# Six more up tiles in seven block products, three transfers moved, and unread products in the selection: a two-block transformer kernel on one core

## The chip, the cores and the metric

The kernel runs on one core of one Trainium2 chip. The metric is the device time of one execution in microseconds (us); a few runs are taken and their median stands for the kernel. A profiled execution gives the trace, and its own time stands beside its span below.

## The reference, cut to what matters

Two transformer blocks one after the other, in float32, on 256 tokens of width 1024. The change lies in the feed-forward part of the first block (two layers) and in the expert selection of the second block (two layers).

```python
# first block, for each of two layers
mod = silu(c) @ w_mod[layer] + b_mod[layer]           # shift, scale and gate vectors, 6 x 1024
h = rmsnorm(x, g_mlp[layer]) * (1 + scale2) + shift2
up = h @ w_up[layer]                                  # 1024 -> 2 x 2816
u, g = up[..., :2816], up[..., 2816:]
g = causal_depthwise_conv(g, conv_w[layer], conv_b[layer])   # three taps along the tokens
x = x + gate2 * ((silu(g) * u) @ w_down[layer])
...
# second block, for each of two layers
aff = softmax(x @ w_router + b_router)                # 16 experts
gate, idx = top_k(aff.T, 32)                          # each expert takes 32 tokens
```

## The kernel before, in words

**Engines.** Each engine runs its own list of instructions in order and waits on semaphores. TensorE (PE) multiplies, VectorE (DVE) and ScalarE (ACT) do the elementwise work, GpSimd (POOL) does some sums, SyncE (SP) issues nearly all transfers.

**Tiles and the ring.** Weights come from memory in tiles of up to 2 MB into a ring of six slots. `_b1_tiles` (line 83) writes the order of the first block's tiles. Before each transfer, SyncE waits until the tile six places ahead in this order has been used (`sp.wait_ge(tile_done, t + 1)`, behind line 680); `tile_done` counts used tiles in the same order, and TensorE raises it. So the place of a tile in the order sets the earliest moment of its transfer. Three transfers are no tiles and stand at fixed places of this loop: the bias copies (line 676) and the router weights (line 678) ahead of up tile 4, and the second layer's attention gate bias (line 682) ahead of up tile 8. SyncE issues in order, and the transfers share one queue.

**Up tiles.** The up projection has eleven tiles a layer. A tile holds 256 columns of `u` and 256 of `g`, and moves in two transfers of 1 MB. A *whole* tile is 32 products of 128x128 weights with 128x256 of the stream, each two instructions in float32 (`up`, line 1266). In the second layer tiles 2 to 10 are multiplied in *seven block products* in place of eight (`up_seven`, line 1304): 56 products of 128x128 with 128x128. These need sums. GpSimd makes the first and third weight sums (`up_sums`, lines 2221 and 2223), VectorE the second (`up_second`, 2790) and the fourth (`up_fourth`, 2796), and once a layer the sums of the stream's rows (`up_rows_sums`, 2779 to 2784). ScalarE copies block 1 out of PSUM (`up_copies`, 1918) and VectorE joins the other six (`up_join`, 2810 to 2816). `UP_WHOLE = (11, 2)` says how many tiles of each layer are whole.

**Convolution.** For each up tile VectorE makes the last tap with its bias (2759) and adds the other two taps (2764), ScalarE takes silu (1927), VectorE multiplies with `u` (2771). That last step is `b1_product_ready`; TensorE waits for it before it overwrites a PSUM bank or reads the product.

**Modulation tiles.** Each of `w_mod`'s tiles (2 MB) is reduced on VectorE by `accumulate` in eight steps (one of line 2381, seven of line 2384, 128x512 each), then summed over partitions by TensorE in `modulation` (line 900 for gates, 903 for the others), and read by `mod_out` (2401, 2403). Sums alternate between two buffers. In the first layer, modulation tiles 10 to 21 follow one each upon up tiles 2 to 10 and down tiles 0 to 2 (`LAGS`): VectorE sums tile 10 + j after product j, and TensorE multiplies it behind up tile j + 2.

**Down tiles.** The down projection has six tiles, also in seven products (line 1332). VectorE makes all its sums (`down_sums`, 2828 to 2837). Tiles 3, 5 and 4 end it together, and their second product needs the sums of all three.

**Selection.** In the second block (second loop over layers), TensorE turns the router's result into logits (`logits`, 1561) and transposes the affinities (`flip_affinity`, 1567). VectorE then finds the 32 largest in four rounds (3175, 3177) and forms slot numbers (3182, 3185), which TensorE transposes (1601, 1603); VectorE copies them (3187). `warm` (line 1573) writes products that nothing reads to a PSUM bank; five stand in these waits before the change, and one behind.

The order on SyncE around the moved transfers:

```python
for t, (L, kind, j) in enumerate(B1_TILES):
    if (L, kind, j) == (0, "up", 4):
        sp.dma_start(copies...)      # bias copies, 2.7 MB
        sp.dma_start(router...)      # 128 KB in rows of 64 bytes
    if (L, kind, j) == (0, "up", 8):
        sp.wait_ge(sems["b1_mix_added"], 4)
        sp.dma_start(gates...)       # 512 KB
    sp.wait_ge(tile_done, t + 1)     # the tile six places ahead is used
```

## Time and profile before

| what | value |
|---|---|
| median of three runs | 1941.82 us (1941.79 to 1944.37) |
| the profiled execution's own time | 1944.36 us |
| its span | 1942.6 us |
| TensorE matmul busy | 1657.2 us (85%) |
| VectorE busy | 708.4 us (36%) |
| ScalarE busy | 283.5 us (15%) |
| GpSimd busy | 143.7 us (7%) |
| bytes read from memory | 594.76 MB |
| TensorE begins the first layer's up stage | 184.92 us |
| one half of a whole up tile (128 of the 256 tokens) | 7.14 us |
| eight transposes of the stream between two halves | 0.87 us |
| first block | 0 to about 769 us |
| second block's experts | from about 924 and from about 1509 us |

In a chain of waits each row is one stretch of work that released the next: its start, its length, and the engine, name and line. A timeline row has start, length, engine, line, operation, shapes and count, and in brackets the idle time before it with what ended it. A windows row gives for each stretch its length, each engine's busy time with instructions, the granted clock (1.00 is 2.4 GHz, 0.50 is 1.2 GHz), the share of time for which the 16 transfer engines were busy, and the rate. PE is TensorE's matmul, PEld its weight loads, SPq SyncE's queue of issues.

### The profile page before, as it was taken

To read this page: it belongs to the slowest core of one execution; us is meant where nothing else is said; L and a number is where in the kernel's file an instruction comes from. 1 tells how busy PE (TensorE), PEld (TensorE's weight loads), DVE (VectorE), ACT (ScalarE), POOL (GpSimd) and SP (SyncE) were. 2 spreads that over 40 slices of the span, in tenths; PEclk is the share of its full clock that TensorE was granted. 3 is DMA by queue.
4 is the path that set the end of the run, shared out by engine and by line. 5 is a ranking of instruction groups with operands and counts; after the bars stand their busy time and mean duration, and the time that the engine had idled before them with its cause. 6 is when DMAs were issued, how large, how long until landed. Compare 5 with 4: busy or idle time off the path is not lost.

```text
span 1942.6 us, 24583 instructions
## 1 busy us (share of the span) xinstructions
PE 1657.2 (85%) x10484; PEld 945.1 (49%) x10484; DVE 708.4 (36%) x1470; ACT 283.5 (15%) x761; POOL 143.7 (7%) x151
## 2 busy tenths in 40 slices
PE   8999999999999999999785766758999785756757
PEld 3455988544579964474432232322574432232322
DVE  1584566977528976273010010101174110010101
ACT  1243000021511001252000010001253000010000
POOL 0011000000213510310000000000220000000000
PEclk9999999999999999999897887979999997987978
DMA  9991888755235643646999999999845999999998
GB/s 353 328 350 59 261 292 298 277 202 187 88 110 187 233 152 125 201 174 241 402 428 430 428 432 425 433 429 409 266 174 216 404 429 430 426 432 427 432 429 352
DMA packets 165957, 599.76 MB, mean 309 GB/s; under 512 B 20977, under 2 KB 79857, under 8 KB 142065
## 3 DMA queue, kind: packets, MB, share of 16 engines
q1 hardware_dynamic: 165630, 598.04, 78.4%
q8 instruction: 61, 1.00, 0.2%
q10 hardware_dynamic: 242, 0.53, 0.1%
q14 instruction: 24, 0.19, 0.0%
HBM read 594.76 MB, written 3.80 MB: 308 GB/s over the span
## 4 chain that ended last, share of the span: by engine, by line
PE 57%; DMA 38%; DVE 3%; ACT 2%; issue 1%; POOL 0%; SPq 0%; DVEq 0%; ACTq 0%
DMA extra<-in_w_down 14%; DMA extra<-in_w_up 12%; DMA extra<-in_w_gate 11%; PE ps L1266 9%; PE ps L1379 6%; PE ps L1332 6%; PE ps L1304 5%; PE ps L1625 5%; PE ps L949 4%; PE ps L1118 4%; PE ps L1517 3%; PE ps L1216 3%; PE ps L1645 1%; DMA ring<-in_w_mod 1%; PE ps L835 1%; PE ps L857 1%
## 5 line engine op out<-in xcount | busy, mean ns | idle before, releaser
L1625 PE MATMUL ps<-ring,wide 128*32 128x256 f32 x2912 | 219.7, 468 | 117.4 <-DMA ring<-in_w_up 72.4
L1625 PEld LDWEIGHTS ps<-ring,wide 128*32 128x32 f32 x2912 | 107.7, 133 | 223.2 <-DMA ring<-in_w_up 81.8
L1645 PE MATMUL ps<-ring,wide 128*32 128x512 f32 x768 | 157.4, 638 | 45.7 <-DMA ring<-in_w_down 45.7
L3212 DVE TENSOR_TENSOR wide<-ps,wide 128x512 f32<-128x512 f32 x16 | 10.7, 670 | 508.8 <-PE ps L1625 508.8
L1266 PE MATMUL ps<-hT,ring 128*128 128x256 f32 (+1 forms) x1088 | 183.8, 330 | 0.0
L1266 PEld LDWEIGHTS ps<-hT,ring 128*128 128x128 f32 x1088 | 166.6, 191 | 17.3 <-issue 2.9
L1625 PE MATMUL ps<-extra,wide 128*32 128x256 f32 x1056 | 91.4, 519 | 63.6 <-DMA extra<-in_w_up 38.7
L1379 PE MATMUL ps<-ring,hT 128*128 128x512 f32 (+2 forms) x320 | 127.3, 555 | 0.4 <-issue 0.4
L1645 PEld LDWEIGHTS ps<-ring,wide 128*32 128x32 f32 x768 | 44.7, 116 | 154.4 <-issue 126.4
L2384 DVE SCALAR_TENSOR_TENSOR extra<-ring,sc,extra 128x512 f32<-128x512 f32 x140 | 109.8, 785 | 5.2
L1625 PEld LDWEIGHTS ps<-extra,wide 128*32 128x32 f32 x1056 | 42.9, 147 | 111.0 <-DMA extra<-in_w_up 42.5
L1379 PEld LDWEIGHTS ps<-ring,hT 128*128 128x128 f32 x320 | 60.3, 190 | 62.2 <-issue 53.4
L949 PE MATMUL ps<-ring,hT 128*128 128x512 f32 x192 | 86.6, 606 | 0.9 <-ACT hT L1771 0.9
L2153 ACT ACTIVATE wide<-ps 128x512 f32<-128x512 f32 x8 | 4.8, 597 | 560.8 <-PE ps L1645 420.2
L3225 DVE COPY wide<-ps 128x512 f32<-128x512 f32 x8 | 5.5, 692 | 203.1 <-PE ps L1645 202.5
L2232 POOL TENSOR_TENSOR sc<-sc,tab 128x1 f32<-128x1 f32 (+1 forms) x18 | 24.5, 1370 | 621.2 <-DVE sc L2329 589.6
L1304 PE MATMUL ps<-hT,ring 128*128 128x128 f32 x576 | 68.7, 275 | 0.0
L1304 PEld LDWEIGHTS ps<-hT,ring 128*128 128x128 f32 x576 | 66.6, 192 | 1.0 <-issue 1.0
L1332 PE MATMUL ps<-ring,wide 128*128 128x512 f32 x136 | 61.6, 595 | 0.0
L1573 PE MATMUL ps<-tab 128*128 128x512 f32 (+1 forms) x116 | 58.5, 643 | 1.2 <-DVE spare L3177 1.2
L949 PEld LDWEIGHTS ps<-ring,hT 128*128 128x128 f32 x192 | 36.3, 193 | 44.8 <-issue 43.4
L1517 PE MATMUL ps<-ring,hT 128*128 128x512 f32 x128 | 56.6, 595 | 0.9 <-ACT hT L2084 0.9
(373 smaller groups left out, 2098.6 us busy)
## 6 DMA issues: line engine op xcount, KB each, us to landing
ring<-in_w_gate SPq DMA_DIRECT2D x24, 4096.0 KB, 31.4
ring<-in_w_down SPq DMA_DIRECT2D x24, 4096.0 KB, 33.6
ring<-in_w_up SPq DMA_DIRECT2D x20, 4096.0 KB, 32.9
ring<-in_w_mod SPq DMA_DIRECT2D x24, 2048.0 KB, 13.4
ring<-in_w_up SPq DMA_DIRECT2D x44, 1024.0 KB, 8.0
extra<-in_w_gate SPq DMA_DIRECT2D x8, 4096.0 KB, 35.1
extra<-in_w_up SPq DMA_DIRECT2D x8, 4096.0 KB, 33.1
ring<-in_w_in SPq DMA_DIRECT2D x13, 2048.0 KB, 12.6
```

Of the source, the lines that this page charges most:

```text
L949: last = mm(ps[bank1(i, c)][:, 0:w], h8[:, k, c * P:(c + 1) * P], wt[:, k, 0:w], start=k == 0, stop=k == KD - 1)
L1118: last = mm(ps[in_bank(m, r)][:, :], lhs[:, g, :], rhs[:, g, :], start=g == 0, stop=g == 3)
L1216: last = mm(ps[OUT_BANK[c, n]][:, :], h8[:, k, c * P:(c + 1) * P], wt[:, k, :], start=k == 2, stop=k == 7)
L1266: last = mm(ps[2 * (j % 2) + half][:, f * T + o:f * T + o + n], wt[:, k, w:w + P], h8[:, k, o:o + n], start=k == 0, stop=k == KD - 1)
L1304: last = mm(ps[UP_BANK[m]][:, half * P:(half + 1) * P], lhs[:, g, half, :], rhs[:, g, :], start=g == 0, stop=g == 3)
L1332: last = mm(ps[DOWN_BANK[m]][:, :], lhs[:, g, :], rhs[:, g, :], start=begin and j == tiles[0] and g == 0, stop=end and j == tiles[-1] and ...
L1379: last = mm(ps[2 * (i % 2) + c][:, 0:w], h8[:, k, c * P:(c + 1) * P], wt[:, k, 0:w], start=k == 0, stop=k == KD - 1)
L1517: last = mm(ps[bank][:, :], h8[:, at_, c * P:(c + 1) * P], wt[:, k, :], start=k == parts[0][0], stop=k == parts[-1][0])
L1573: mm(ps[bank][:, 0:cols_], ident, tab[:, 0:cols_], start=True, stop=True)
L1625: last = mm(ps[2 * part + e // 2][j * CAP:(j + 1) * CAP, e % 2 * 2 * P:(e % 2 + 1) * 2 * P], xsT[:, k, e * CAP:(e + 1) * CAP], expert_row( ...
L1645: last = mm(ps[6 + n][e * CAP:(e + 1) * CAP, :], hidT[:, e, k, :], expert_row(n0, e, k)[:, n * N:(n + 1) * N], start=k == 0, stop=k == KD - 1)
L2384: stt(acc[:, q % 2, :], wt[:, k, :], csil[:, k:k + 1], acc[:, q % 2, :], ALU.mult, ALU.add)\
```

## The change

- `UP_WHOLE` becomes `(5, 2)`: up tiles 5 to 10 of the first layer go in seven products as in the second. The functions that were for the second layer alone take the layer as a parameter; GpSimd's `up_sums` stands ahead of the router's gains now.
- The first tap with its bias goes from VectorE (two instructions of line 2759) to ScalarE (`tap`, two activations with scale and bias), in both layers. `conv(j)` is left with four VectorE instructions. In a step of seven products `conv(j - 1)` stands ahead of the joins of tile j.
- At the first seven-product tile the second weight sum comes ahead of the row sums, and both ahead of the convolution of the tile before.
- Modulation tiles of the first layer get new places in the order (`FOLD_AFTER`), sums at new places on VectorE (10 to 13 in the residual stretch, then `SUM_WHOLE`, `SUM_FIRST`, `SUM_PARTS`), reads at new places (`READ_AFTER`), three sum buffers in place of two, and other PSUM banks.
- The bias copies and router weights are issued ahead of up tile 8, not 4; the gate bias ahead of up tile 2, not 8.
- Three unread products are added to each selection.

```diff
-UP_WHOLE = (11, 2)
+UP_WHOLE = (5, 2)
+FOLD_AFTER = ({("out", 1): (10, 11), ("up", 1): (12, 13), ("up", 2): (14, 15), ("up", 3): (16,), ("up", 4): (17, 18),
+               ("up", 7): (19,), ("up", 9): (20,), ("down", 2): (21,)}, {("up", 6): (0,), ("up", 7): (1,)})
+READ_AFTER = ({1: (12, 13), 2: (14, 15), 3: (16,), 8: (19,), 10: (20,)}, {6: (0,), 7: (1,)})
+SUM_WHOLE = {0: (14,), 1: (15,), 2: (16, 17), 3: (18,)}
+SUM_FIRST = ({5: (19, range(0, 2)), 6: (19, range(4, 6)), 7: (20, range(0, 2)), 8: (20, range(4, 6))}, {})
+SUM_PARTS = ({5: (19, range(2, 4)), 6: (19, range(6, 8)), 7: (20, range(2, 4)), 8: (20, range(6, 8))},
...
-                if (L, kind, j) == (0, "up", 4):
+                if (L, kind, j) == (0, "up", 8):
                     sp.wait_ge(sems["rpb_loaded"], 16)
...
-                if (L, kind, j) == (0, "up", 8):
+                if (L, kind, j) == (0, "up", 2):
                     sp.wait_ge(sems["b1_mix_added"], 4)
...
                         elif m == 5:
-                            pe.wait_ge(*s.at("b1_product_ready", 2))
+                            pe.wait_ge(*s.at("b1_product_ready", first - first % 2))
+                        elif m == 3:
+                            pe.wait_ge(*s.at("b1_product_ready", first - 1 + first % 2))
...
                 route(1, range(4, KD)).then_inc(s.up("b2_router_done"), 1)
+                warm(7, 1, T)
                 pe.wait_ge(*s.at("b2_logits_ready", 1))
                 logits(1)
                 flip_affinity(0)
+                warm(7, 1)
+                warm(7, 1, P)
                 flip_affinity(1)
...
+                def tap(j):
+
+                    y = sm[:, j % 2, :].rearrange("p (f t) -> p f t", f=2)
+                    act.wait_ge(*up_block(s, L, 4, j))
...
+                    for f in range(2):
+                        av(y[:, f, :], gp[:, f, :], ACT.Identity, scale=cc1(L, "conv_w", 2 * FCH + 2 * j + f),
+                           bias=cc1(L, "conv_b", 2 * j + f)).then_inc(s.up("b1_up_by_act" if f else None), 1)
...
                 out_residual(0, 0)
+                if L == 0:
+                    accumulate(10)
                 out_residual(0, 1)
                 norm_stream(which, 0)
                 out_residual(1, 0)
                 evac_stream(which, 0, 24)
+                if L == 0:
+                    accumulate(11)
                 out_residual(1, 1)
                 norm_stream(which, 1)
                 evac_stream(which, 1, 24)
+                if L == 0:
+                    accumulate(12)
+                    mod_out(10)
+                    accumulate(13)
+                    mod_out(11)
...
+                first = UP_WHOLE[L]
+                for j in range(first - 1):
+                    conv(j)
+                    up_gated(j)
+                    if L == 0:
+                        for q in SUM_WHOLE[j]:
+                            accumulate(q)
+                up_second(first)
+                up_rows_sums()
                 if L == 0:
-                    mod_out(EARLY[L] + UPT - LAGS[L])
+                    mod_out(17)
+                    mod_out(18)
+                for j in range(first, UPT):
+                    if j in SUM_FIRST[L]:
+                        accumulate(*SUM_FIRST[L][j])
+                    conv(j - 1)
+                    up_join(j, UP_READS[:1])
+                    up_fourth(j)
+                    up_gated(j - 1)
+                    if j in SUM_PARTS[L]:
+                        accumulate(*SUM_PARTS[L][j])
+                    if j == UPT - 1:
+                        down_sums(0)
+                    up_join(j, UP_READS[1:])
+                conv(UPT - 1)
+                up_gated(UPT - 1)
+                down_sums(1)
                 down_sums(2)
                 down_sums(3)
                 if L == 0:
-                    accumulate(EARLY[L] + UPT)
-                    mod_out(EARLY[L] + UPT + 1 - LAGS[L])
+                    accumulate(21)
```

## Rows read from the trace of the kernel before

**Rows 1.** The page: the span, and its 40 slices of transfers (share busy, rate)
```profile
span 1942.6 us, 24583 instructions
...
DMA  9991888755235643646999999999845999999998
GB/s 353 328 350 59 261 292 298 277 202 187 88 110 187 233 152 125 201 174 241 402 428 430 428 432 425 433 429 409 266 174 216 404 429 430 426 432 427 432 429 352
```

**Rows 2.** Chain of waits, first layer's up and down stage (start us, us, what)
```profile
242.87 0.86 PE ps L900 x2
243.72 13.81 PE ps L1266 x64
257.54 0.79 PE ps L903 x8
...
346.49 12.23 PE ps L1332 x28
...
371.73 0.42 DVE extra L2828
...
393.99 20.87 PE ps L1332 x48
```

**Rows 3.** Timeline of TensorE, second layer's first seven-product tiles
```profile
585.10 3.74 PE L1304 MATMUL ps<-hT,ring 128*128 128x128 f32 x32
...
594.35 2.05 PE L1304 MATMUL ps<-extra 128*128 128x128 f32 x16 [1.27 <-DVE wide L2771]
...
599.81 3.74 PE L1304 MATMUL ps<-hT,ring 128*128 128x128 f32 x32
...
612.32 3.74 PE L1304 MATMUL ps<-hT,ring 128*128 128x128 f32 x32
```

**Rows 4.** Timeline of SyncE's issues, first layer
```profile
189.98 17.79 SPq L678 DMA_DIRECT2D router<-in_w_router  x1
207.82 3.06 SPq L705 DMA_DIRECT2D ring<-in_w_up  x2
```

**Rows 5.** Windows of the first layer (busy us, clock, transfer share, GB/s)
```profile
187.00:198.00 11.00, 11.00 (x101) 11.00 (x100) 2.28 (x6) 2.92 (x7) 0.54 (x1) 1.00 1.06 372
198.00:208.00 10.00, 10.00 (x92) 10.00 (x91) 0.73 (x2) 0.00 (x0) 0.00 (x0) 1.00 0.93 262
208.00:212.00 4.00, 4.00 (x39) 4.00 (x38) 3.20 (x8) 0.63 (x1) 0.57 (x1) 1.00 0.58 94
245.00:256.00 11.00, 11.00 (x53) 9.68 (x52) 7.66 (x12) 0.63 (x1) 0.00 (x0) 1.00 1.03 361
```

**Rows 6.** Windows of the first selection
```profile
909.90:913.40 3.50, 1.62 (x6) 0.62 (x6) 2.09 (x11) 2.41 (x4) 0.00 (x0) 0.97 1.00 424
913.40:920.20 6.80, 6.27 (x8) 2.62 (x9) 4.88 (x21) 3.32 (x3) 0.00 (x0) 0.51 1.00 422
```

**Rows 7.** Timeline, both selections: unread products and VectorE's wait behind them
```profile
913.93 6.72 PE L1573 MATMUL ps<-tab 128*128 128x512 f32 x8 [0.59 <-DVE spare L3177]
...
921.02 0.19 DVE L3187 COPY sc<-ps 128x32 f32<-128x32 f32 x1 [2.43 <-PE ps L1603]
...
1506.30 0.19 DVE L3187 COPY sc<-ps 128x32 f32<-128x32 f32 x1 [0.85 <-PE ps L1603]
```

**Rows 8.** Timeline of VectorE, second layer's seven-product tiles
```profile
587.97 1.22 DVE L2790 TENSOR_TENSOR extra<-extra,ring 128x1024 f32<-128x1024 f32 x1
589.29 1.00 DVE L2759 TENSOR_SCALAR spare<-ps,fixed 128x256 f32<-128x256 f32 x2
...
614.47 1.79 DVE L2764 SCALAR_TENSOR_TENSOR spare<-extra,fixed,spare 128x255 f32<-128x255 f32 x4
...
616.63 1.23 DVE L2796 TENSOR_TENSOR ring<-ring,extra 128x1024 f32<-128x1024 f32 x1
```

**Rows 9.** Groups of VectorE: modulation steps, 599.8 to 700, then 200 to 340 us
```profile
L2384 DVE SCALAR_TENSOR_TENSOR extra<-ring,sc,extra 128x512 f32<-128x512 f32 x14 | 15.0, 1075 | 0.7
...
L2384 DVE SCALAR_TENSOR_TENSOR extra<-ring,sc,extra 128x512 f32<-128x512 f32 x68 | 51.2, 753 | 2.4
```

More of the change, by code:

```diff
@@ L90, in _b1_tiles @@
                 tiles += [(0, "mod", q) for q in MOD_AT[i]]
-        tiles += [(l, "out", j) for j in range(2)]
-        late = MODS[l][EARLY[l]:]
-        steps = [(l, "up", j) for j in range(UPT)] + [(l, "down", j) for j in range(NDOWN)]
-        for n, t in enumerate(steps):
+        tiles.append((l, "out", 0))
+        for t in [(l, "out", 1)] + [(l, "up", j) for j in range(UPT)] + [(l, "down", j) for j in range(NDOWN)]:
             tiles.append(t)
-            if LAGS[l] <= n < len(late) + LAGS[l]:
-                tiles.append((late[n - LAGS[l]][0], "mod", late[n - LAGS[l]][1]))
+            tiles += [(MODS[l][q][0], "mod", MODS[l][q][1]) for q in FOLD_AFTER[l].get(t[1:], ())]
     return tiles
@@ L124, with _up_acts @@
 TAB = {}
+def _up_acts(l):
+    first = UP_WHOLE[l]
+    acts = [(what, j) for j in range(first - 1) for what in ("tap", "silu")]
+    for j in range(first, UPT):
+        acts += [("tap", j - 1), ("copy", j), ("silu", j - 1)]
+    return acts + [("tap", UPT - 1), ("silu", UPT - 1)]
+UP_ACTS = [_up_acts(l) for l in range(DEPTH)]
+UP_SEVEN = [UPT - UP_WHOLE[l] for l in range(DEPTH)]
 def _tab():
@@ L1317, in _ @@
                         up(j, 0, T)
-                    if 0 <= j - LAGS[L] < late:
-                        modulation(EARLY[L] + j - LAGS[L])
+                    folds(("up", j))
                 pe.wait_ge(*s.at("b1_product_ready", UPT - 1))
@@ L1349, in _ @@
                     last.then_inc(tile_done, 1)
-                    if UPT + j - LAGS[L] < late:
-                        modulation(EARLY[L] + UPT + j - LAGS[L])
+                    folds(("down", j))
                 for j in DOWN_TAIL:
@@ L1927, in _, with up_copies @@
                     av(pT[:, j % 2, :], sm[:, j % 2, :], ACT.Silu).then_inc(s.up("b1_up_by_act"), 1)
+                def up_copies(j):
+                    act.wait_ge(*up_block(s, L, 1, j))
+                    if j >= UP_WHOLE[L] + 2:
+                        act.wait_ge(*s.at("b1_product_ready", j - 1))
+                    for c in range(2):
+                        av(up_joined(j)[:, :, 0, c * P:(c + 1) * P], ps[UP_BANK[1]][:, 0:T].rearrange("p (h t) -> p h t", h=2),
+                           ACT.Copy).then_inc(s.up("b1_up_by_act" if c else None), 1)
+                for what, j in UP_ACTS[L]:
+                    if what == "tap":
+                        tap(j)
+                    elif what == "silu":
+                        silu(j)
+                    else:
+                        up_copies(j)
                 if L == DEPTH - 1:
@@ L2389, in mod_out @@
                     t = B1_AT[(l, "mod", i)]
-                    b = MOD_BANK if L or t > B1_AT[(L, "down", 0)] else 7 - q % 2 if q in MOD_AT[LAST_IN] else 4 + q % 2
+                    b = mod_bank(L, q)
                     if L == 0 and q < FAST:
@@ new lines, in _ @@
+                if L == 0:
+                    mod_out(17)
+                    mod_out(18)
+                for j in range(first, UPT):
+                    if j in SUM_FIRST[L]:
[9 more added lines that the diff above has]
+                    up_join(j, UP_READS[1:])
```

207 lines of the change are left out of this document (96 added, 111 removed).

## The prediction

> **What bounds the kernel now.** Read the page first: the span is 1942.6 us and the row of transfers is at its ceiling only in the two stretches in which the experts' weights stream; the first 900 us are not filled by them [rows 1]. So a microsecond saved ahead of 900 us moves the whole stream to the left. The second view is the chain of waits over the first layer's up and down stage: it is TensorE without a gap to the end of the second down tile, one whole up tile (line 1266) being 13.81 us, with a modulation product of 0.86 or 0.79 us between two tiles; only at 371.73 does VectorE take over, until TensorE starts again at 393.99 [rows 2]. The third is the timeline of the second layer, where tiles of the same size already go in seven products: in steady state one takes 612.32 - 599.81 = 12.51 us [rows 3]. The fourth is what feeds the first layer: SyncE's issues and the rate of the transfers [rows 4, 5]. The last is the selection, where unread products run at half the full clock [rows 6, 7].
>
> The profiled execution took 1944.36 us, 1.8 more than its span; the median of the runs is 1941.82, 2.5 less. Differences of span are put on the median. 0.2% of it, 3.9 us, is about what a measurement can tell from no change.
>
> **The change, part by part.** *Six tiles in seven products.* 13.81 - 12.51 = 1.3 us [rows 2, 3], times six is 7.8 us less TensorE. ScalarE's copy and taps, GpSimd's sums and VectorE's joins come on top; what they cost is whether they are late, below.
>
> *Modulation tiles 19 and 20.* Their products move from behind down tiles 0 and 1 into the up stage: 0.79 us each, no difference in the sum. Taken alone the up stage would end 7.8 - 1.6 = 6.2 us earlier, at 340.3 where it was 346.49 [rows 2].
>
> *The down stage.* VectorE's last sums end at 393.99, 47.5 us after the stage begins; they restart when down tile 1 is done, 25.2 us in, because two modulation products lie before that [rows 2]. Without them two tiles of 12.1 us make 24.3, so this chain ends some 1.0 us earlier relative to the stage's start. Modulation sum 21 stays in it, so the stall of 2 to 3 us before 393.99 stays: VectorE is late next, as before.
>
> *Sums 10 to 13 ahead of the convolutions.* Each is eight steps, 6.0 us, on VectorE in the residual and norm stretch, where it mostly waits for TensorE. TensorE's clock of the new stage, from the table: 184.92 + 7.14 + 0.87 (transposes) + 7.14 = 200.1, modulation products 10 and 11 to 201.8, two more half tiles to 216.1, products 12 and 13 to 217.6. VectorE has sums 12 and 13 and their reads done at about 208.4, up tile 0 ends at 208.9, and taps, silu and product take some 4 us: product 0 comes at 213 and tile 2 wants it at 217.6; tile 2's own transfer lands near 209. Cost nothing; if the cover is gone, each sum costs 6.0 us at most.
>
> *The transfers.* This is where I expect most of the gain to go. A transfer waits until the tile six places ahead in the order is done. In the new order tile 2 of up waits for modulation tile 10, which TensorE finishes at about 201, and from there the queue does not run dry: up 2, modulation 14, 15, up 3, 16, up 4, 17, 18, up 5, 6, 7, 19 are all released before the queue reaches them. A pair of an up and a modulation tile (4.2 MB) moves at 361 to 372 GB/s [rows 5], so a tile takes 5.65 to 5.8 us; with a late end on some of the 16 engines it may be 6.2. I take 5.75. From 202.3, twelve tiles put modulation tile 19 at 271. VectorE wants its first two steps at the head of the step of up tile 5, before conv 4, the first join and the fourth sum. From landing to the fourth sum are two steps (1.3 us) and the stretch 614.47 to 617.86 of the second layer [rows 8]: 4.7 us, and product 4 0.6 more. TensorE starts tile 5 at 217.6 + 3 x 13.8 + 4.1 (five modulation products) = 263.1 and wants both 9 us into it, at 272; it gets them at 276 to 277. **Stall one: 4 us.**
>
> Behind tile 19 come the bias copies and the router weights, which the change puts ahead of up tile 8. Before, they sat right ahead of the transfer issued at 207.82: the queue moved at 262 GB/s and then at 94 GB/s for the 14 us from 198 to 212, and SyncE's issue of the router took 17.79 us, so everything behind it on SyncE waits too [rows 4, 5]. Then up 8, up 9 and modulation tile 20: 14 + 3 x 5.75 = 31 us after tile 19. Tile 20 lands at about 302.5 (301 by the fast rate, 309 by the slow one). Tile 6 ends at 263.1 + 2 x 12.5 + 4 = 292.1; VectorE is through its joins and reaches modulation 20's first two steps (ahead of conv 6) at 293 to 294 and stands in order behind the wait: conv 6, join and fourth sum of tile 7 are queued there, and TensorE waits for that sum at 300 to 301. It gets it at 302.5 + 4.7 = 307.2. **Stall two: 6 us.** From there to the down stage no other transfer is late: two products of tile 7 (3.6 us), three tiles of 12.5, two modulation products of 0.8. The down stage then starts at 307.2 + 3.6 + 37.5 + 1.6 = 349.9, against 346.49: 3.4 later instead of 6.2 earlier. With the 1.0 of the down stage, **the first layer loses 2.4 us**. By the fast rate it loses 1, by the slow one 9; with no backlog at all it wins 7.2.
>
> The gate transfer (0.5 MB) moves ahead of up 2 and lies in the queue before 202: nothing.
>
> *Layer two.* ScalarE now makes the first tap, and the order is second sum, row sums, conv 1 instead of row sums, second sum, conv 1. Seven-tile 2 took 599.81 - 585.10, 2.2 us over the steady 12.51, and the one large wait in it is for product 1 [rows 3, 8]. Taking out the second sum (1.2) and the two taps (1.0) brings product 1 to 592.1, where TensorE wants it at 592.2. **Minus 2.2**, and nothing else in that layer changes on TensorE. ScalarE's two taps (some 1 us) are late by a fraction only at the last tile, where line 1332 wants product 10 with 2 us to spare.
>
> *Selection.* Between 909.9 and 913.4 TensorE is busy 1.62 of 3.5 us at a granted clock of 0.97; in the 6.8 us after that the granted clock is 0.51, that is 1.2 GHz, and four unread products (eight instructions) last 6.72 us. VectorE waits 2.43 us for the product behind them; in the second selection 0.85 us [rows 6, 7]. The change adds unread products of 256 columns ahead of the second logits and 512 and 128 ahead of the second flip, some 1.5 us at 2.4 GHz, in gaps of 0.5 and 1.4 us. If the clock holds, the waits shrink to the 0.55 us that the two small products need: **minus 1.9 and minus 0.3**. They hide in the gaps; at 1.2 GHz they would cost 0.8 us a selection instead. The bounds are therefore -2.2 and +1.6. I take -2.2, since the activity ahead of the fall nearly doubles.
>
> By the Trainium skill ("TensorE: Matmul & The Clock Gate", The HAM clock gate) the gate judges activity on its own free-running timing, not on the program's. By that rule shifting the program can move the fall to other instructions whatever the added products do, and the sum would be 2.2 us less good. No row here shows one execution with another phase.
>
> Sum: 2.4 - 2.2 - 2.2 = -2.0 us, **1939.8 us**.
>
> **VectorE beside GpSimd.** In the second layer the fourteen modulation steps of line 2384 last 1075 ns in the mean where, without GpSimd at work, they last 753 [rows 9]. The new steps lie where GpSimd has paused, so I price them at 0.8; at 1.075, a tile of the first layer with four steps fills VectorE for some 13 us against 12.5, 0.5 us each for four tiles, 2 us at most. The Trainium skill ("SBUF — State Buffer", Who interferes with whom) says that a VectorE instruction with two inputs in SBUF and a reading GpSimd one exclude each other for the whole instruction. The trace's mean agrees.
>
> **The rivals.**
> A. *The transfers are in time.* If transfers overlap better than one after another, tile 20 lands before 296 and only stall one or nothing is left. Then the first layer wins 3.2 to 7.2, and the whole 8 to 12: 1930 to 1934. For it: the page's rate reaches 430 GB/s in the experts' stretch [rows 1]. Against: no stretch with these packets is above 372 [rows 5]. Chance 0.22.
> B. *The queue falls further behind, slower than before.* One mechanism, at VectorE's wait for modulation tile 20 ahead of conv 6. Each microsecond that it lands after 302.5 is one on the path. At 304.5 the gain is gone, and from 308.5 the kernel is over 0.2% slower. With 6.2 us a tile and 16 us for copies and router it lands at 309 to 310: first layer +9.5, total +5, 1947. For it: every 2 MB counts from the slowest of the 16 engines, and landings are later than the mean rate says. Against: gaps in the release let the slow engine catch up. Chance 0.20.
> C. *The clock does not hold* and all else as forecast: 1942.0, or 1943.6 with the added products in the way. Chance 0.18.
> The forecast itself, within 3 us: 0.40.
>
> **How the numbers follow.** Most of A, and the part of the forecast in which tile 20 lands by 300.5, is faster by over 0.2%: 0.36. The slower half of B with a clock that does not hold gives 0.19. The rest, 0.45, is no difference. The range takes the forecast, C, most of B and the nearer part of A: 1931.5 to 1947.
>
> **What would show it.** A TensorE tile of 12.5 us in the first layer and two long ones, of 16 to 17 us (up 5) and 18 (up 7); VectorE idle before line 2384's step, released by the transfer of a modulation tile, twice; transfer share near 1 from 202 to 300; the router's issue after 261; tile 2 of the second layer at 12.5 us; VectorE's wait before line 3187's copy at 0.6 us in both selections. The forecast is wrong if the down stage starts before 346 or after 353, or if the granted clock falls in the selection.

## The result, and the profile after

The changed kernel takes **1952.91 us**, median of five runs (1949.92 to 1953.8), beside 1944.08 us for the kernel before in the same comparison. The ratio is 1.0047, 95% interval 1.0036 to 1.0058: slower by 0.47%, some 9 us, outside the range of the prediction. The profiled execution took 1953.05 us with a span of 1951.0, 8.4 more than the 1942.6 of before, so the two profiles carry the whole difference.

It is easiest to find by milestones of TensorE, the moments at which it begins a stage. The columns are the profile before, the profile after, what the stretch gained or lost, and what the prediction had for it.

| stretch | before | after | difference | forecast |
|---|---|---|---|---|
| first layer's down stage begins | 346.35 | 355.14 | +8.8 | +3.4 |
| from there to its last group of blocks | 70.1 | 68.9 | -1.15 | -1.0 |
| from there to the second layer's up stage | 139.2 | 142.5 | +3.3 | 0 |
| second layer's nine seven-product tiles | 116.8 | 116.2 | -0.5 | -2.2 |
| all behind the first block, the selections in it | 1175.4 | 1173.5 | -1.9 | -2.2 |

The last group of the down stage is at 416.43 before and 424.07 after, the up stage at 555.64 and 566.58. The stretches not listed are equal to 0.01 us. The sum is +8.4, and against the forecast's -2.0 it leaves 10.4 us to explain: 5.4 in the first row, 3.3 in the third, 1.7 in the fourth. The first row counts from the start of the span, and executions of one kernel come to the up stage at different times: 184.76 us in the profile before, 183.96 in the one after, 181.3 to 184.0 in the four profiles of the kernel after. From the first up tile to the down stage are 161.6 us before and 171.2 after: the stage itself is 9.6 us longer.

The page's row of transfers is as full as the forecast has it: the fifth slice of the rates has 344 GB/s where it had 261, the sixth 320 where it had 292 [rows 1].

```profile
span 1951.0 us, 25339 instructions
...
DMA  9992996545325742744999999999944999999998
GB/s 352 334 341 75 344 320 238 194 168 194 124 87 174 248 165 86 244 173 197 402 431 428 425 433 426 432 430 410 288 173 199 406 427 432 425 431 427 432 430 351
```

TensorE's timeline of the first layer has the forecast's two long tiles. Up tile 5 begins at 263.71, tile 7 at 297.59; in each the sixth block waits for VectorE. The bracket is the idle time.

```profile
261.01 1.02 PE L940 MATMUL ps<-extra,tab 128*128 128x512 f32 x2
262.79 1.05 PE L943 MATMUL ps<-tab,extra 128*128 128x1 f32 x8 [0.77 <-DVE extra L2454]
263.71 3.82 PE L1355 MATMUL ps<-hT,ring 128*128 128x128 f32 x32
...
270.94 1.95 PE L1355 MATMUL ps<-extra 128*128 128x128 f32 x16
278.61 3.78 PE L1355 MATMUL ps<-hT,ring 128*128 128x128 f32 x16 [5.72 <-DVE wide L2845]
282.18 3.07 PE L1355 MATMUL ps<-extra,ring 128*128 128x128 f32 x16
285.09 3.74 PE L1355 MATMUL ps<-hT,ring 128*128 128x128 f32 x32
...
297.59 3.74 PE L1355 MATMUL ps<-hT,ring 128*128 128x128 f32 x32
...
310.56 2.60 PE L1355 MATMUL ps<-hT,ring 128*128 128x128 f32 x16 [3.87 <-DVE ring L2870]
312.96 3.04 PE L1355 MATMUL ps<-extra,ring 128*128 128x128 f32 x16
...
355.14 1.02 PE L1382 MATMUL ps<-ring,wide 128*128 128x512 f32 x2
```

A group of 16 products that elsewhere begins 1.79 us before its successor takes 3.57 and 2.91 us behind the first stall, 2.40 and 2.87 behind the second. The windows say why: the granted clock, 0.93 and 1.00 in the two gaps themselves, is at its lower level (0.50, 1.2 GHz) for most of both stretches behind them.

```profile
278.60:285.10 6.50, 6.49 (x33) 6.49 (x34) 4.67 (x8) 0.00 (x0) 0.00 (x0) 0.54 0.75 158
310.50:316.00 5.50, 5.44 (x35) 5.47 (x35) 5.02 (x8) 0.00 (x0) 1.04 (x1) 0.69 0.00 0
```

Against 1.79 for a group that is 2.9 us lost behind the first stall and 1.7 behind the second. What VectorE did ahead of the second stands in its own timeline, with GpSimd's below it:

```profile
303.33 0.48 DVE L2451 TENSOR_SCALAR extra<-ring,sc 128x512 f32<-128x512 f32 x1 [4.66 <-DMA ring<-in_w_mod]
303.86 0.75 DVE L2454 SCALAR_TENSOR_TENSOR extra<-ring,sc,extra 128x512 f32<-128x512 f32 x1
304.52 3.68 DVE L2838 SCALAR_TENSOR_TENSOR spare<-extra,fixed,spare 128x255 f32<-128x255 f32 x4
308.13 0.41 DVE L2890 TENSOR_TENSOR extra<-ps,extra 128x256 f32<-128x256 f32 x1
308.57 1.84 DVE L2870 TENSOR_TENSOR ring<-ring,extra 128x1024 f32<-128x1024 f32 x1
...
```

```profile
305.05 2.87 POOL L2280 TENSOR_TENSOR extra<-ring 128x512 f32<-128x512 f32 x2 [6.29 <-PE ps L1355]
307.89 3.65 POOL L2282 TENSOR_TENSOR ring<-ring 128x512 f32<-128x512 f32 x2
```

Modulation tile 20 landed at 303.3 (forecast 302.5). But the four taps took 3.68 us, not the 1.79 of [rows 8], and the fourth sum 1.84, not 1.23; TensorE's block could start at 310.6 instead of 307.2. Behind the first stall's landing the same four taps ran beside GpSimd's sums too, which were at work from 271.25 to 276.88. There they read PSUM and not two tiles of SBUF, the on-chip memory, and took what they take alone:

```profile
274.45 1.77 DVE L2838 SCALAR_TENSOR_TENSOR spare<-ps,fixed,spare 128x255 f32<-128x255 f32 x4
```

In the selection the rows that answer to [rows 6] and [rows 7] have a full clock, and eight product instructions last 4.37 us, not 6.72:

```profile
922.00:928.00 6.00, 5.11 (x13) 1.60 (x12) 5.33 (x26) 5.14 (x4) 0.00 (x0) 1.00 0.99 421
```

```profile
921.05 1.24 PE L1618 MATMUL ps<-tab 128*128 128x512 f32 x4
...
924.32 4.37 PE L1618 MATMUL ps<-tab 128*128 128x512 f32 x8 [0.59 <-DVE spare L3247]
```

### The profile page after: what moved, and what is told of

The parts are those of the page before. It is cut to its first block, busy times and chain, and to the rows that moved or that the text cites. A ratio compares the mean times of both kernels' runs of the same rounds, so it can differ in the third digit from the quotient of the medians.

```text
span 1951.0 us, 25339 instructions
## 1 busy us (share of the span) xinstructions
PE 1654.6 (85%) x10784; PEld 951.7 (49%) x10784; DVE 736.6 (38%) x1484; ACT 310.1 (16%) x817; POOL 178.9 (9%) x175
## 4 chain that ended last, share of the span: by engine, by line
PE 52%; DMA 38%; DVE 5%; ACT 2%; SPq 1%; issue 1%; POOL 0%; DVEq 0%; ACTq 0%
DMA extra<-in_w_down 14%; DMA extra<-in_w_up 12%; DMA extra<-in_w_gate 11%; PE ps L1424 6%; PE ps L1355 6%; PE ps L1382 6%; PE ps L1673 5%; PE ps L1306 5%; PE ps L989 4%; PE ps L1158 4%; PE ps L1562 3%; PE ps L1256 3%; DMA ring<-in_w_mod 2%; PE ps L1693 1%; DVE extra L2454 1%
## 5 line engine op out<-in xcount | busy, mean ns | idle before, releaser
L1355 PE MATMUL ps<-hT,ring 128*128 128x128 f32 x960 | 117.3, 279 | 9.6 <-DVE wide L2845 5.7
L1355 PEld LDWEIGHTS ps<-hT,ring 128*128 128x128 f32 x960 | 113.1, 195 | 10.9 <-DVE wide L2845 5.9
L1306 PE MATMUL ps<-hT,ring 128*128 128x128 f32 (+1 forms) x704 | 100.1, 304 | 0.0
L1306 PEld LDWEIGHTS ps<-hT,ring 128*128 128x128 f32 x704 | 94.1, 191 | 6.7 <-issue 1.9
L2454 DVE SCALAR_TENSOR_TENSOR extra<-ring,sc,extra 128x512 f32<-128x512 f32 x112 | 95.1, 849 | 4.5
L989 PE MATMUL ps<-ring,hT 128*128 128x512 f32 x192 | 86.6, 606 | 0.9 <-ACT hT L1819 0.9
L2280 POOL TENSOR_TENSOR extra<-ring 128x512 f32<-128x512 f32 x30 | 43.6, 1474 | 194.0 <-PE ps L1355 126.8
L1618 PE MATMUL ps<-tab 128*128 128x512 f32 (+2 forms) x128 | 59.3, 590 | 1.2 <-DVE spare L3247 1.2
```

The source lines that it names most:

```text
L989: last = mm(ps[bank1(i, c)][:, 0:w], h8[:, k, c * P:(c + 1) * P], wt[:, k, 0:w], start=k == 0, stop=k == KD - 1)
L1306: last = mm(ps[2 * (j % 2) + half][:, f * T + o:f * T + o + n], wt[:, k, w:w + P], h8[:, k, o:o + n], start=k == 0, stop=k == KD - 1)
L1355: last = mm(ps[UP_BANK[m]][:, half * P:(half + 1) * P], lhs[:, g, half, :], rhs[:, g, :], start=g == 0, stop=g == 3)
L1618: mm(ps[bank][:, 0:cols_], ident, tab[:, 0:cols_], start=True, stop=True)
L2454: stt(total, wt[:, k, :], csil[:, k:k + 1], total, ALU.mult, ALU.add)\
```

## The experiments

Sixteen runs follow: twelve changed kernels and four repetitions of the kernels before and after. The theory at the start: two stalls of TensorE at VectorE's waits for modulation tiles 19 and 20, each with a stretch of half clock behind it. The rival: transfers or VectorE's load set the pace, and the place of the waits does not matter. The main readings of the profiles are in one table at the end of this section.

**The copies and the router later** (`e1_router_late`).

```diff
-                if (L, kind, j) == (0, "up", 8):
+                if (L, kind, j) == (0, "down", 0):
```

> Kernel after, with the two transfers (bias copies, router) sent ahead of down tile 0 instead of up tile 8. Theory (two stalls, each followed by a stretch at half clock): modulation tile 20 lands some 14 us earlier, the second stall (3.9 us at 310.6) and the 1.8 us that its blocks took longer go, the first stall (5.7 us and 3.1 us) stays: 5 to 6 us less than after, 1.0015 to 1.002 of before. Rival (the queue is only behind somewhere else): the down tiles then come late, the down stage waits and the time stays at after's.

1946.83 us, ratio 1.0022 (1.0013 to 1.0032): 6 us under after, the larger end of what was expected. The second stall is gone and the first, now 6.73 us, stays. Tile 20 is there when VectorE wants it, and the taps behind it take their usual time, because they are over before GpSimd starts its next sums at 303.85:

```profile
298.69 1.79 DVE L2838 SCALAR_TENSOR_TENSOR spare<-extra,fixed,spare 128x255 f32<-128x255 f32 x4
```

So the slow taps of the kernel after come of the wait: the late tile pushes them onto GpSimd's sums.

**The sums behind the first join** (`e2_sums_behind_join`).

```diff
-SUM_FIRST = ({5: (19, range(0, 2)), 6: (19, range(4, 6)), 7: (20, range(0, 2)), 8: (20, range(4, 6))}, {})
+SUM_FIRST = ({}, {})
-SUM_PARTS = ({5: (19, range(2, 4)), 6: (19, range(6, 8)), 7: (20, range(2, 4)), 8: (20, range(6, 8))},
+SUM_PARTS = ({5: (19, range(0, 4)), 6: (19, range(4, 8)), 7: (20, range(0, 4)), 8: (20, range(4, 8))},
```

> Kernel after, with the sums of modulation tiles 19 and 20 that stood at the head of VectorE's part of seven-product tiles 5 to 8 put behind the first join of the same tile (four steps there instead of two and two). Theory: VectorE no longer stands in front of a transfer with the taps and the fourth sum behind it, so both stalls of TensorE go with their slow clock: 5.7 + 3.1 + 3.9 + 1.8 = 14.5 us less than after, some 1940 us (0.997 of before), less if the two parts not split make the joins late. Rival (the lost time is VectorE's load and the collision with GpSimd, not the place of the wait): the stalls move to the joins, at most 4 us less than after.

1950.53 us, ratio 1.0035 (1.0020 to 1.0049). The rival is right. The two long stalls go and six short ones come, at the second or the fourth sum of tiles 6 to 9, 7.8 us together:

```profile
282.13 2.02 PE L1355 MATMUL ps<-spare,extra 128*128 128x128 f32 x16 [1.05 <-DVE extra L2864]
288.59 2.02 PE L1355 MATMUL ps<-hT,ring 128*128 128x128 f32 x16 [0.86 <-DVE ring L2870]
...
298.24 2.74 PE L1355 MATMUL ps<-spare,extra 128*128 128x128 f32 x16 [2.27 <-DVE extra L2864]
...
313.99 2.02 PE L1355 MATMUL ps<-spare,extra 128*128 128x128 f32 x16 [0.49 <-DVE extra L2864]
```

The granted clock falls again behind the two waits of 2.27 us (0.64 and 0.65 over the next 5 us), which makes these tiles longer still. Four steps of a sum behind the join are more than VectorE has room for. Two ahead of the taps and two behind the join do fit as long as the tile has landed: in `e1_router_late` up tiles 6 to 8 have four steps each and take 12.5 us. Ahead of the taps the two steps stand in the 1.2 us in which VectorE otherwise waits for ScalarE's first tap, and before GpSimd's sums.

**Both edits** (`e3_both`).

> Both edits. Theory: no more than e2 alone, since either cure removes the second stall, and e2 the first too: within 2 us of e2. Rival (the transfers themselves bound the up stage, their 98 per cent share of the queue): e3 is faster than e2 by 4 us or more, for up tiles 8 and 9 come 10 us earlier.

1951.38 us, ratio 1.0043 (1.0030 to 1.0057), the same as `e2_sums_behind_join` within the intervals. With the four steps together behind the join VectorE's work binds, wherever the router stands.

**The selection alone** (`e4_before_plus_products`). The kernel before, with only the three unread products.

```diff
+                warm(7, 1, T)
                 pe.wait_ge(*s.at("b2_logits_ready", 1))
                 logits(1)
                 flip_affinity(0)
+                warm(7, 1)
+                warm(7, 1, P)
```

> Kernel before, with only the three unread products of the selection. Theory: the granted clock holds behind the first selection, 1.9 us there and 0.3 in the second layer: 2.2 us less than before, ratio 0.9989. Rival: the products only fill the wait and the clock falls all the same, ratio 1.000.

1941.93 us, ratio 0.9993 (0.9983 to 1.0002): 2.1 us less, as expected, though the interval reaches 1. The clock row decides: 1.00 through the stretch that answers to [rows 6]. Of the eighteen profiles of this study the sixteen with the three products have no fall in the first selection, the two without have one. This part of the change works, but what it gives depends on the execution: 1.9 us against the profile of before that the prediction read, 0.7 against its repetition (below).

**Sums spread three to a tile, tile 20 back in the down stage** (`f1_spread`). On top of the first experiment's edit:

```diff
-               ("up", 7): (19,), ("up", 9): (20,), ("down", 2): (21,)}, {("up", 6): (0,), ("up", 7): (1,)})
+               ("up", 8): (19,), ("down", 1): (20,), ("down", 2): (21,)}, {("up", 6): (0,), ("up", 7): (1,)})
-SUM_FIRST = ({5: (19, range(0, 2)), 6: (19, range(4, 6)), 7: (20, range(0, 2)), 8: (20, range(4, 6))}, {})
+SUM_FIRST = ({}, {})
-SUM_PARTS = ({5: (19, range(2, 4)), 6: (19, range(6, 8)), 7: (20, range(2, 4)), 8: (20, range(6, 8))},
+SUM_PARTS = ({6: (19, range(0, 3)), 7: (19, range(3, 6)), 8: (19, range(6, 8))},
...
                 down_sums(1)
+                if L == 0:
+                    accumulate(20)
                 down_sums(2)
                 down_sums(3)
                 if L == 0:
                     accumulate(21)
+                    mod_out(20)
```

> Kernel after with three edits in the first layer: the bias copies and the router ahead of down tile 0; modulation tile 19 taken after up tile 8 instead of 7, its eight steps put behind the joins of tiles 6, 7 and 8 as 3, 3 and 2; modulation tile 20 taken after down tile 1, with its sums behind the second down sums, where the kernel before has them. Theory (VectorE was both waiting at transfers and, at four steps of a sum in each tile, full): neither stands now, the six tiles take 12.5 us each and the down stage starts at 339 to 342 us instead of 346.5 before and 355.3 after; with the selection's 2.2 us the whole is 8 to 10 us under before, ratio 0.995 to 0.996. Rival (the saturated transfers bound the up stage in any order): TensorE waits at up tiles 8 to 10 by name of the weights, the down stage starts at 347 or later, ratio 0.999 or more.

**1937.88 us, ratio 0.9974 (0.9964 to 0.9983)**: faster than before, by 5.6 us where 8 to 10 were expected (its profiled execution has 7.7 us less span). In the profile the down stage starts at 339.55, as expected; no tile waits, each takes 12.5 us:

```profile
276.12 3.74 PE L1355 MATMUL ps<-hT,ring 128*128 128x128 f32 x32
...
288.63 3.74 PE L1355 MATMUL ps<-hT,ring 128*128 128x128 f32 x32
...
301.14 3.74 PE L1355 MATMUL ps<-hT,ring 128*128 128x128 f32 x32
```

**The same, and the second layer's modulation tile 11 a tile later** (`f2_spread_both`).

```diff
-{("up", 6): (0,), ("up", 7): (1,)})
+{("up", 6): (0,), ("up", 8): (1,)})
...
-             {3: (0, range(0, 3)), 4: (0, range(3, 6)), 5: (0, range(6, 8)), 6: (1, range(0, 4)), 7: (1, range(4, 8))})
+             {3: (0, range(0, 3)), 4: (0, range(3, 6)), 5: (0, range(6, 8)), 6: (1, range(0, 3)), 7: (1, range(3, 6)), 8: (1, range(6, 8))})
```

> The kernel of f1_spread, with the second layer's modulation tile 11 taken after up tile 8 instead of 7 and its steps spread 3, 3, 2 instead of 4, 4. Theory: the 1.7 us for which TensorE waited at that tile go: 1.5 to 2 us under f1_spread. Rival (VectorE is the pace of the whole stage of seven-product tiles there, by its own joins): the stall only moves to a later tile, no difference from f1_spread.

**1933.85 us, ratio 0.9954 (0.9938 to 0.9971)**: the best version, 9.6 us under before. The seven-product tiles of the second layer take 114.3 us instead of 116.2, the 1.9 expected; the other 2 us by which the medians differ belong to no place that the edit touches. The stall that went is this one of the kernel after, with VectorE's four steps of 1.5 us ahead of it. One tile earlier the steps started 0.6 us later than before and then ran longer beside GpSimd (4.6 us instead of 3.7); that put these four 1.5 us late. Half of the 0.6 is the first tap that the change moved to ScalarE: VectorE's taps start 1.22 us behind its last join, all of it a wait for ScalarE, where with its own first tap (0.74) they started 0.91 behind.

```profile
673.78 1.13 PE L940 MATMUL ps<-extra,tab 128*128 128x512 f32 x2 [1.68 <-DVE extra L2454]
```

```profile
663.00 1.79 DVE L2838 SCALAR_TENSOR_TENSOR spare<-extra,fixed,spare 128x255 f32<-128x255 f32 x4 [1.22 <-ACT spare L1970]
...
667.69 6.03 DVE L2454 SCALAR_TENSOR_TENSOR extra<-ring,sc,extra 128x512 f32<-128x512 f32 x4
```

**The second layer's edit alone** (`k1_layer2_tile`). The last diff on the kernel after.

> Kernel after, with only the second layer's modulation tile 11 after up tile 8 and its steps 3, 3, 2. Theory: 1.7 us for which TensorE waited at that tile go, 1.5 to 2 us under after. Rival: the median difference between f2_spread_both and f1_spread, 4.0 us, is all of this edit.

1950.34 us, ratio 1.0049 (1.0027 to 1.0071): the medians can't tell 2 us here. The profile has the stage at 114.3 us again, so the edit is worth 1.9 us, not 4.

**Unread products in the two stalls** (`h1_products_in_stalls`, `h2_fewer_products`).

```diff
                     for m in UP_STEPS:
+                        if L == 0 and m == 3:
+                            for _ in range({5: 12, 7: 8}.get(j, 0)):
+                                mm(ps[MOD_BANK][:, :], ones, tab[:, 0:N], start=True, stop=True)
```

> Kernel after, with 12 products that nobody reads in TensorE's first stall (up tile 5) and 8 in the second (up tile 7). Theory (3.1 and 1.8 us of the loss are the half clock behind the stalls, not the stalls): the clock stays at full behind both, the blocks of 16 take 1.8 us again, 4 to 5 us under after, with the stalls' own 9.6 us still lost. Rival (the blocks were slow because the operands came late, or a clock fall comes elsewhere in its place): same as after within 1 us.

1954.65 us, ratio 1.0052 (1.0035 to 1.0069). My products were sized wrong: one is two instructions and takes 0.87 us, so twelve took 10.46 us in a gap of 5.7. The clock did stay at 1.00 behind them, and from the sixth block of up tile 7 (314.69) to the down stage (357.57) were 42.9 us, where the kernel after took 44.6. With six and four:

> Kernel after, with 6 and 4 unread products in the two stalls instead of 12 and 8 (one takes 0.87 us, as the run before this one showed, so 5.2 and 3.5 us, within the stalls of 5.7 and 3.9). Theory: the stalls stay, the 4.9 us of half clock behind them go, 4 to 5 us under after. Rival (a fall of the clock that is avoided here comes later): the half-clock time ahead of the selection is as long as after's 19 us, and the time too.

1952.55 us, ratio 1.0052 (1.0034 to 1.0069): no gain, and this is the most instructive miss. TensorE's timeline (line 1340 is the unread products):

```profile
272.56 5.31 PE L1340 MATMUL ps<-tab 128*128 128x512 f32 x12
278.47 2.05 PE L1358 MATMUL ps<-hT,ring 128*128 128x128 f32 x16 [0.59 <-DVE wide L2848]
282.15 3.74 PE L1358 MATMUL ps<-hT,ring 128*128 128x128 f32 x32
...
303.59 3.60 PE L1340 MATMUL ps<-tab 128*128 128x512 f32 x8
310.79 3.64 PE L1358 MATMUL ps<-hT,ring 128*128 128x128 f32 x16 [3.60 <-DVE ring L2873]
```

Behind the first stall the clock holds and up tile 6 begins at 282.15 instead of 285.09. The second gap is longer now, and the clock falls behind it again. Those 3 us are then waited in full at the second stall, which ends at 310.79 as it ended at 310.56 after: modulation tile 20 still lands at 303.1. So the first stall's slow clock costs nothing in the kernel after, where the second stall follows; up to the end of that stall the landing of tile 20 and VectorE's work behind it decide.

**The spread sums, with the router where the change put it** (`j1_spread_router_early`). The kernel of 1937.88 us without its first edit.

> The kernel of f1_spread, but with the bias copies and the router where the change put them, ahead of up tile 8. Theory (what was lost hung on where VectorE waits, and now only up tiles 8 to 10 and modulation tile 19 are behind the copies, with slack): same as f1_spread within 1 us. Rival (the queue was the cause and the sums only its victim): up tile 8 or modulation tile 19 comes late, 4 us or more above f1_spread.

1946.79 us, ratio 1.0021 (1.0010 to 1.0032), 9 us above it. The rival is right: behind the copies and the router modulation tile 19 lands at 290.66, VectorE waits 8.52 us for it, and TensorE 3.59 us for the second sum of tile 7.

```profile
290.66 0.49 DVE L2451 TENSOR_SCALAR wide<-ring,sc 128x512 f32<-128x512 f32 x1 [8.52 <-DMA ring<-in_w_mod]
```

**Only modulation tile 20 taken out of the up stage** (`n1_tile20_late`), its sums where `f1_spread` has them.

```diff
-               ("up", 7): (19,), ("up", 9): (20,), ("down", 2): (21,)}, {("up", 6): (0,), ("up", 7): (1,)})
+               ("up", 7): (19,), ("down", 1): (20,), ("down", 2): (21,)}, {("up", 6): (0,), ("up", 7): (1,)})
```

> Kernel after, with only the first layer's modulation tile 20 taken out of the up stage: after down tile 1, its sums behind the second down sums, as before the change. The copies, the router, tile 19 and its place stay. Theory (the sixth block of up tile 7 starts at 310.6 to 310.8 whatever happened before it, because tile 20 lands at 303.3 and VectorE needs 7 us from there): that stall and its slow clock go, the first stall stays, up tile 7 ends near 310, the down stage starts at 348 to 350 instead of 355.3, 5 to 6 us under after. Rival (up tiles 8 and 9, behind the router, would be late by themselves): the down stage starts at 353 or later.

1946.36 us, ratio 1.0015 (1.0005 to 1.0024), 6.5 us under after. The second stall is gone, the first (5.69 us) is as it was, and the down stage starts at 345.15. Up tiles 8 and 9 were never late behind the router.

**GpSimd held back** (`n2_gpsimd_holds`).

```diff
                     if j > UP_WHOLE[L]:
                         pool.wait_ge(*up_block(s, L, 7, j - 1))
+                    if L == 0 and j in (6, 8):
+                        pool.wait_ge(*up_summed(s, L, "s4", j - 1))
```

> Kernel after, with GpSimd's sums of up tiles 6 and 8 of the first layer held back until VectorE's fourth sum of the tile before. Theory (VectorE's taps take 3.7 instead of 1.8 us and its fourth sum 1.8 instead of 1.2 because GpSimd's sums run beside them): alone they take 1.8 and 1.2 us, the sixth block of up tile 7 starts at 308 instead of 310.6, and 2 to 3 us of the time go unless GpSimd then comes late for the next tile's second sum. Rival (the taps are slow for their own reasons, the transfers for one): the same durations as in after, and the time up by what GpSimd is later.

The profile has VectorE's instructions at the lengths they have alone:

```profile
300.43 0.49 DVE L2453 TENSOR_SCALAR extra<-ring,sc 128x512 f32<-128x512 f32 x1 [5.43 <-DMA ring<-in_w_mod]
300.95 0.75 DVE L2456 SCALAR_TENSOR_TENSOR extra<-ring,sc,extra 128x512 f32<-128x512 f32 x1
301.62 1.78 DVE L2840 SCALAR_TENSOR_TENSOR spare<-extra,fixed,spare 128x255 f32<-128x255 f32 x4
303.32 0.42 DVE L2892 TENSOR_TENSOR extra<-ps,extra 128x256 f32<-128x256 f32 x1
303.77 1.22 DVE L2872 TENSOR_TENSOR ring<-ring,extra 128x1024 f32<-128x1024 f32 x1
```

From landing to TensorE's block are 305.14 - 300.43 = 4.7 us, the prediction's figure to a tenth; in the kernel after it is 7.2, in its three further profiles 7.2, 8.3 and 7.2. The collision is shown. It isn't a cure: GpSimd is later for what follows (TensorE waits 0.86 us in tile 8 and 0.69 in tile 9), and the runs give 1951.83 us, ratio 1.0038 (1.0024 to 1.0052), 1 us under after in the median, which the intervals don't tell from nothing.

**The same kernels again**, for the 3.3 us of the second layer's attention, in which nothing was changed.

> Kernel after, unchanged, profiled again. Theory (the 3.3 us lost in the second layer's attention are a fall of the clock that the same instructions meet in some executions and not in others): the stretch from the end of the first layer to the second layer's up stage takes 139.2 to 139.5, 141 or 142.5 us, not always 142.5. Rival (the new timing of the first layer sets it): 142.5 us each time. Either way the sixth block of up tile 7 starts near 310.6.

> As a1_after_again: the same kernel once more, for the same two readings.

> As a1_after_again: the same kernel a third time, for the same two readings.

> Kernel before, unchanged, profiled again. Theory: if the fall in the second layer's attention is a matter of the single execution, it can come here too (139.2 us in the profile shown, 142.5 with it). Rival: it belongs to the change, 139.2 us again.

One execution each: 1950.29, 1952.03 and 1949.7 us after, 1943.21 before. The stretch takes 142.5, 139.5, 139.5 and 139.2 us. The same rows in the first profile of the kernel after and in the third repetition:

```profile
508.04 0.92 PE L1076 MATMUL ps<-extra 32*128 32x128 f32 x8 [0.69 <-ACT extra L1855]
...
510.60 1.54 PE L1117 MATMUL ps<-wide,extra 128*128 128x64 f32 x6
511.93 2.02 PE L1089 MATMUL ps<-tab 128*128 128x512 f32 x2
```

```profile
507.79 0.92 PE L1076 MATMUL ps<-extra 32*128 32x128 f32 x8 [0.69 <-ACT extra L1855]
...
509.97 0.88 PE L1117 MATMUL ps<-wide,extra 128*128 128x64 f32 x6
510.69 1.08 PE L1089 MATMUL ps<-tab 128*128 128x512 f32 x2
```

The gap ahead, 0.69 us, is the same; the clock falls behind it in one execution of this kernel and not in another. It belongs to the execution.

Two other readings move between executions in the same way. The down stage's stretch to its last group of blocks (second row of the first table) is 68.9 us in three of the four profiles of the kernel after and 70.6 in the fourth, where the clock falls behind a stall of 1.98 us. And in the repetition of the kernel before, VectorE waits no longer for its product in the first selection than it does with the three unread products, though the clock falls there too, where in [rows 7] it waits 2.43 us; in the second selection it waits 1.37 us instead of 0.85.

```profile
918.80 0.19 DVE L3187 COPY sc<-ps 128x32 f32<-128x32 f32 x1 [0.70 <-PE ps L1603]
```

Readings of the profiles, in us. "Up 5 to down" runs from the start of up tile 5 to the start of the down stage, with two late modulation products in it; f1_spread, f2_spread_both, j1_spread_router_early and n1_tile20_late have one; before it was 88.2, with six. "Attention" is the stretch of the third row of the first table, "layer 2" that of the fourth.

| kernel | up 5 to down | attention | layer 2 | ratio |
|---|---|---|---|---|
| after | 91.4 | 142.5 | 116.2 | 1.0047 |
| e1_router_late | 85.6 | 139.5 | 116.2 | 1.0022 |
| e2_sums_behind_join | 89.4 | 139.2 | 116.2 | 1.0035 |
| e3_both | 88.3 | 139.2 | 116.2 | 1.0043 |
| f1_spread | 76.0 | 139.2 | 116.2 | 0.9974 |
| f2_spread_both | 76.0 | 139.2 | 114.3 | 0.9954 |
| h1_products_in_stalls | 94.1 | 142.5 | 116.2 | 1.0052 |
| h2_fewer_products | 91.8 | 139.5 | 116.2 | 1.0052 |
| j1_spread_router_early | 84.2 | 140.9 | 116.2 | 1.0021 |
| k1_layer2_tile | 92.9 | 141.2 | 114.3 | 1.0049 |
| n1_tile20_late | 83.3 | 139.2 | 116.2 | 1.0015 |
| n2_gpsimd_holds | 89.5 | 141.1 | 116.2 | 1.0038 |

The order by ratio follows the first column. e3_both stands out of it, and its profiled execution was the shortest of its six; after, h1, h2 and k1 are not told apart by their intervals.

## Why the prediction was wrong

**The mechanism was right**: tiles of 12.5 us where nothing waits, the queue without slack, two waits of VectorE at modulation tiles 19 and 20, each with a stall of TensorE, in the tiles it named. Tile 19 was there at 272.4 (forecast 271), tile 20 at 303.3 (302.5), the down stage is 1.15 us shorter (1.0) in the profile shown, seven-tile 2 of the second layer takes 12.5 us as forecast. Two hits are partly luck. The selection gave 1.9 us (2.2), but against the profile before that had the dearer of two falls. And up tile 7 took 18.2 us as forecast (18) because two errors met: up tile 5 took 21.4 instead of 16 to 17, so the stall in tile 7 was 3.9 us and not 6, with a slow clock behind it. What failed are three terms.

**"VectorE beside GpSimd", priced at nothing: 2.5 us.** (Tile 20's landing adds 0.8 more; counted from the start of the up stage it was 1.8 late, for TensorE began the stage 1.0 us earlier than the table's 184.92.) The step said that GpSimd has paused where the new steps lie, and it looked at the modulation steps alone. What collided were the instructions queued behind them, taps and fourth sum, with GpSimd's sums for the next tile: 7.2 us from landing to block instead of 4.7. The held-back GpSimd shows it, and the kernel with the router later, whose taps do not wait, has them clear of GpSimd. The bound of 2 us for all four tiles was passed in one of them.

**No price for the clock behind a stall: 1.9 us of the same row.** From the second stall's end the down stage came 44.6 us later (310.56 to 355.14) where I had 42.7. The two slow groups are 1.7 of these 1.9, and where twelve and eight unread products kept the clock up the same stretch took 42.9. The profile of before had the pattern in front of me: a gap of TensorE, then the lower clock, in the selection of [rows 6]. I used it for the selection alone. The first stall's slow clock, 2.9 us, cost nothing, as the six unread products show: time lost ahead of a wait that ends with a transfer is not lost twice. The forecast's own rule for the first stall, that its 4 us delay tile 7 and shorten the second, was the same rule.

**Layer two, -2.2 instead of -0.5.** The gain at its first tile came. What I said of the rest, that "nothing else in that layer changes on TensorE" and that ScalarE's taps are late only at the last tile, failed: VectorE waits 1.22 us for them in five tiles running, the last steps of modulation tile 11 start 1.5 us later against the same product, and beside GpSimd they last 1.5 us each. TensorE waits 1.68 us at that product. Spreading the steps takes the wait away; that the moved tap began it is read from the rows, and no run has the tap back on VectorE.

The remaining 3.3 us are in no term: two of four profiled executions of the kernel after have 3.0 of them and two haven't, and no row of before showed a second phase. The first layer and the second layer's stall make 5.4 + 1.7 = 7.1 us of the 10.4 by which the profile misses the forecast. Whether the fall in the attention is more frequent after than before stays open; the three profiles with the first block as it was before have none, which is too few to say.

Rival B, the queue that falls further behind, had the right sign and size (+9.5 in the first layer, measured +7.6) by the wrong route: the tile landed 0.8 us late, not 7. A reader who took its time for confirmation would have moved the router. That gains 6 us, because tile 20 is then there in time and VectorE's work behind it doesn't meet GpSimd; taking tile 20 out of the stage gains the same with the router where it is.

Rival C fell: the clock holds in the first selection in all sixteen profiles with the products.

## What to carry to other kernels

When a change puts an engine's wait for a transfer ahead of work that another engine needs, price what is queued behind the wait at the durations it has beside whatever runs there then, not at those it has alone. A stall can have a second price, the clock behind it, but only the last stall ahead of the next wait that is set from outside pays it. Count an engine's room per tile before giving it pieces, and look at where in the tile the room is: here three steps of a sum behind the join fitted beside a seven-product tile and four didn't, while two ahead of the taps and two behind did. With that count kept and the bulky side transfers out of the stage, the same rewrite went from a loss of 0.47% to a gain of 0.46%. Profile both kernels more than once before a difference of 2 or 3 us goes into a forecast: one profile of before had 1.7 us in the first selection that its repetition hadn't.

## What the hardware showed that I had not expected

- Four taps of VectorE, two inputs each, took 3.68 us beside GpSimd's sums and 1.78 with GpSimd held back; a fourth sum of 1024 columns 1.84 and 1.22; a step of a modulation sum up to 1.5 against 0.75. The Trainium skill ("SBUF — State Buffer", Who interferes with whom) has such a VectorE instruction and a GpSimd one shut each other out for a whole instruction; these rows agree in that the instructions with both inputs in SBUF are the slow ones, and don't show for how long each is shut out. Four taps with one input in PSUM took 1.77 us beside GpSimd.
- TensorE's granted clock fell to 1.2 GHz behind the gaps of 5.7 us and of 3.9 to 5.1 us in every profile of the kernel after, and behind gaps of 0.25 and 0.69 us in the second layer's attention in two of the four, with a loss of 3.0 us. Behind gaps near 2.3 us it fell twice in `e2_sums_behind_join` and not in `n2_gpsimd_holds`. The Trainium skill ("TensorE: Matmul & The Clock Gate", The HAM clock gate) says that the gate runs on its own timing and not on the program's; the repetitions agree, and they are the row that the prediction said it lacked.
- Twelve unread products of 512 columns took 10.46 us at the full clock, 0.87 each, and kept the clock up as six did.
